# Dilated attention in a decoder trunk: both heads per query block, values stationary, output feature-major, one staging buffer

## The reference

```python
h = rmsnorm(x, g_mix)
qa, ka, va, qr, kr, vr, gr, ga, gb = split(h @ w_in)
# A: 3 groups x 8 heads of 64; windows (128,1), (512,4), (2048,16)
for each group: out_g, lse_g = dilated_group_attention(qa, ka, va)
y_A = (sum over groups of softmax(lse)_g * out_g) @ w_a
# B: retention, 4 heads, keys of 128, values of 256
y_B = (silu(gr) * groupnorm(retention(qr, kr, vr))) @ w_b
x = x + (sigmoid(ga) * y_A + sigmoid(gb) * y_B) @ w_o
x = x + square(relu(rmsnorm(x) @ w_up)) @ w_down
```

## Time and profile before

| what | value |
|---|---|
| median of 3 runs | 1989.29 us (1988.87 to 1989.97) |
| the profiled execution's own time | 1988.87 us |
| its span in the profile | 1987.1 us |
| PE busy | 1959.6 us, 99% of the span |
| mean granted clock of PE | 0.997 |
| DVE, ACT, POOL busy | 1106.3, 728.8, 90.7 us |
| DMA | 177.8 MB, 89 GB/s over the span |

### The profile page before, as it was taken

How to read it: one execution, slowest core, us unless ns; L and a number is a source line. 1 busy time by engine, 2 the same in 40 slices (tenths; PEclk the granted TensorE clock), 3 DMA queues, 4 the chain that set the end, 5 groups by cost and what they waited for, 6 DMA issues and landing times.

```text
span 1987.1 us, 26972 instructions
## 1 busy us (share of the span) xinstructions
PE 1959.6 (99%) x9580; PEld 1648.8 (83%) x9580; DVE 1106.3 (56%) x1716; ACT 728.8 (37%) x1146; POOL 90.7 (5%) x71
## 2 busy tenths in 40 slices
PE   7999999999999999999999999999999999999999
PEld 6988888887888888888889888888878888888887
DVE  5465664748446635354635474747564575445355
ACT  5144435355223413233422435344532233223233
POOL 0010110100000000000001110202000000000000
PEclk9999999999999999999999999999999999999999
DMA  5321222212333232322232222222122233232321
GB/s 173 111 91 44 89 69 84 84 51 76 100 101 106 86 106 87 103 98 92 98 117 91 81 74 63 90 63 90 35 95 95 95 106 106 85 106 84 106 85 64
DMA packets 203900, 177.80 MB, mean 89 GB/s; under 512 B 9776, under 2 KB 194224, under 8 KB 203568
## 3 DMA queue, kind: packets, MB, share of 16 engines
q1 hardware_dynamic: 203536, 176.52, 27.6%
q10 hardware_dynamic: 288, 0.28, 0.0%
HBM read 174.55 MB, written 2.23 MB: 89 GB/s over the span
## 4 chain that ended last, share of the span: by engine, by line
PE 81%; DVE 11%; issue 5%; ACT 2%; POOL 1%; DVEq 0%; DMA 0%; ACTq 0%; POOLq 0%; SPq 0%
PE pj L1155 21%; PE pj L1153 21%; PE pj L1154 21%; DVE w_lo L717 3%; DVE swp L809 2%; PE yo L1259 2%; PE rb L1286 2%; DVE swp L807 1%; DVE probT L878 1%; PE sc L1236 1%; PE pt L1246 1%; PE sc L1202 1%; PE sc L1204 1%; PE sc L1203 1%; PE rb L1272 1%
## 5 line engine op out<-in xcount | busy, mean ns | idle before, releaser
L1153 PE MATMUL pj<-h_hi,w_hi 128*128 128x512 f32 x1408 | 559.2, 397 | 0.0
L1155 PE MATMUL pj<-h_hi,w_lo 128*128 128x512 f32 x1408 | 548.6, 390 | 0.0
L1154 PE MATMUL pj<-h_lo,w_hi 128*128 128x512 f32 x1408 | 548.1, 389 | 0.0
L418 ACT CAST w_hi<-w_raw 128x1024 fp32r<-128x1024 f32 x330 | 329.9, 1049 | 371.0 <-PE pj L1155 277.6
L717 DVE TENSOR_TENSOR w_lo<-w_raw,w_hi 128x1024 fp32r<-128x1024 f32 x330 | 397.9, 1247 | 94.8 <-ACT w_hi L418 94.0
L1154 PEld LDWEIGHTS pj<-h_lo,w_hi 128*128 128x128 f32 x1408 | 264.5, 188 | 57.2 <-issue 2.4
L1153 PEld LDWEIGHTS pj<-h_hi,w_hi 128*128 128x128 f32 x1408 | 264.4, 188 | 56.6 <-issue 2.4
L1155 PEld LDWEIGHTS pj<-h_hi,w_lo 128*128 128x128 f32 x1408 | 264.2, 188 | 55.6
L1153 PE MATMUL pj<-z_hi,w_hi 128*128 128x512 f32 x640 | 249.6, 390 | 0.0
L1154 PE MATMUL pj<-z_lo,w_hi 128*128 128x512 f32 x640 | 249.2, 389 | 0.0
L1155 PE MATMUL pj<-z_hi,w_lo 128*128 128x512 f32 x640 | 249.2, 389 | 0.0
(11 more groups left out here) (185 smaller groups left out, 2348.4 us busy)
## 6 DMA issues: line engine op xcount, KB each, us to landing
w_raw<-in_w_in SPq DMA_DIRECT2D x152, 512.0 KB, 4.2
w_raw<-in_w_up SPq DMA_DIRECT2D x64, 512.0 KB, 4.1
w_raw<-in_w_down SPq DMA_DIRECT2D x64, 512.0 KB, 3.9
w_raw<-in_w_b SPq DMA_DIRECT2D x16, 512.0 KB, 3.8
w_raw<-in_w_o SPq DMA_DIRECT2D x16, 512.0 KB, 3.9
w_raw<-in_w_a SPq DMA_DIRECT2D x16, 256.0 KB, 3.0
x_nat<-in_x SPq DMA_DIRECT2D x2, 1024.0 KB, 6.4
tables<-in_tables SPq DMA_DIRECT2D x2, 1024.0 KB, 7.1
```

What stands on the lines that cost most here:

```text
L418: nc.scalar.copy(w_hi[s][:, c], raw[s][:, c]).then_inc(hi_done, 1)
L1153: nc.tensor.matmul(out, w_hi[s][:, wc], acts[0], start=first, stop=False)
L1154: nc.tensor.matmul(out, w_hi[s][:, wc], acts[1], start=False, stop=False)
L1155: return nc.tensor.matmul(out, w_lo[s][:, wc], acts[0], start=False, stop=last)
```

## The change

- **Both heads per query block.** A pass is now one query block with both heads: 4 passes j a pair. `prob`, `probT` and `pt` hold both heads. `masked`, `exp` work through 4 pieces each; `turn` makes 6 or 8 transposes; the passes are spread wider over the 12 steps (`turn(0)` now in step 5).
- **Values stationary.** `values` holds 64 columns of `vA` stationary and streams 128 columns of `probT`. Head 0 writes PSUM partitions 0 to 63, head 1 partitions 64 to 127, so the output is feature-major. The number of products is the same. `U` is feature-major and `u_copy` runs once for each block.
- **Statistics per pair.** After each pair SP exchanges that pair's residue statistics, DVE works out the shares (`shares`, `shares_end`, with an `Exp` on ACT, `share_power`, between), PE turns them to 4 rows with 4 small products (`share_rows`), ACT copies the rows (`rows_copy`), SP writes them to DRAM and reads them back broadcast over the partitions (`spread_rows`), and `y_sum` on DVE scales both sides of `U` and adds them.
- **Removed:** `factors`, `u_scale`, `y_turn`, `y_copy`, `y_add` at the gates.
- **One staging buffer.** `raw` is one buffer. A half of a unit is loaded once the same half of the unit before it has been split. In query/key units a half now holds one output tile, so that a tile needs its half alone.
- In PE's program the loop over the pairs is written out, which makes the column offsets of `vA` constants. The split of z, `ret_scale` and the gate copies are reordered at the gates. Retention's scratch moves from `prob` and `probT` to `scr`.

```diff
+            def load(n, halves, opens=None):
+
+                for i, (dst, src) in enumerate(halves):
+                    sp.wait_ge(lo_done, (n - 1) * 2 + i + 1 + UNIT_CREDIT)
+                    if opens and i == 0:
+                        sp.sem_inc(opens, 1)
+                    sp.dma_start(dst, src).then_inc(landed[i], 16)
...
+            def pair(v, *ts):
+
+                d = raw[:].rearrange("p (o k c) -> p o k c", o=2, c=P)
+                return [(d[:, o], v[:, :, t, :]) for o, t in enumerate(ts)]
...
+            def half_unit(n, v, t):
+
+                d = raw[:].rearrange("p (k c) -> p k c", k=KT)
+                sp.wait_ge(lo_done, (n - 1) * 2 + 1 + UNIT_CREDIT)
+                sp.dma_start(d[:, 0:KA, :], v[:, 0:KA, t, :]).then_inc(landed[0], 16)
+                sp.wait_ge(lo_done, (n - 1) * 2 + 2 + UNIT_CREDIT)
+                sp.sem_inc(landed[1], 16)
 
...
+                def exchange(J):
+
+                    sp.wait_ge(att_exp, J * 16 + 16)
+                    sp.dma_start(scratch.rearrange("(p r) c -> p r c", r=TB),
+                                 stats[:, TB:2 * TB].rearrange("p b w h -> p b (w h)")).then_inc(stats_sent, 16)
+                    sp.wait_ge(stats_sent, J * 16 + 16)
+                    sp.dma_start(other[:].rearrange("p b w h -> p b (w h)"),
+                                 scratch.rearrange("(b p) c -> p b c", p=P)).then_inc(other_in, 16)
+
+                def spread_rows(J):
+
+                    sp.wait_ge(rows_out, J + 1)
+                    sp.dma_start(row_scratch, rows).then_inc(rows_sent, 16)
+                    sp.wait_ge(rows_sent, J * 16 + 16)
+                    by_head = row_scratch.rearrange("(w h) s -> h w s", h=2)
+                    for hh in range(2):
+                        src = by_head[hh].unsqueeze(0).to_broadcast([DH, 2, S])
+                        sp.dma_start(spread_share[hh * DH:(hh + 1) * DH], src).then_inc(share_in, 16)
...
+                    last_two(i)
+                    after = first_four(l * LU + P0 + (i + 1) * P_U, w_in_next, i)
+                    load_pair(*after[0])
+                    load_pair(*after[1])
+                    exchange(J)
+                    load_pair(*after[2])
+                    load_pair(*after[3])
+                    spread_rows(J)
+                last_two(PAIRS - 1)
+
...
+                    load(n + 0, cols(w_in_u[l], COL_GA // 256 + p))
+                    load(n + 1, cols(w_in_u[l], COL_GB // 256 + p))
+                    if first:
+                        first()
+                    load(n + 2, cols(w_b_u[l], p))
+                    half_unit(n + 3, w_a_u[l], p)
+                    if last:
+                        last()
+
+                gates(0, lambda: exchange(l * PAIRS + PAIRS - 1), lambda: spread_rows(l * PAIRS + PAIRS - 1))
...
+                def share_power(J):
+                    act.wait_ge(share_diff, J * 3 + 3)
+                    nc.scalar.activation(share[:], share[:], ACT.Exp).then_inc(share_exp, 1)
+
+                def rows_copy(J):
+                    act.wait_ge(rows_turned, J + 1)
+                    nc.scalar.copy(rows, rb[0:4, :]).then_inc(rows_out, 1)
...
+                    ret_square(J, 0)
                     gate_sig(i, 1)
-                    act.wait_ge(att_pv, J * 8 + 8)
                     ret_square(J, 1)
+                    share_power(J)
                     rot_in(i + 1, 0, 0)
                     ret_root(J)
                     rot_in(i + 1, 0, 1)
-                    for u in range(1, GROUPS):
-                        ahead(l, P0, P_U, i + 1, u)
-                        rot_in(i + 1, u, 0)
-                        rot_in(i + 1, u, 1)
+                    ahead(l, P0, P_U, i + 1, 1)
+                    rot_in(i + 1, 1, 0)
+                    rows_copy(J)
+                    rot_in(i + 1, 1, 1)
+                    ahead(l, P0, P_U, i + 1, 2)
+                    rot_in(i + 1, 2, 0)
+                    rot_in(i + 1, 2, 1)
...
+                def u_copy(J, j):
+
+                    dve.wait_ge(att_pv, J * 4 + j + 1)
+                    if j == 0:
+                        dve.wait_ge(y_done, J + 1)
+                    c = slice(j * P, j * P + P)
+                    own, by_res = yo[:, 0:P], yo[:, P:2 * P]
+                    nc.vector.tensor_scalar(U[:, 0, c], own, 1.0, None, ALU.mult).then_inc(u_out, 1)
+                    nc.vector.tensor_scalar(by_residue(U[:, 1, :])[:, j], by_res, 1.0, None, ALU.mult).then_inc(u_out, 1)
...
+                def shares(J):
+
+                    own, res = stats[:, 0:TB], other[:]
+                    dve.wait_ge(other_in, J * 16 + 16)
+                    nc.vector.tensor_tensor(least[:], own[:, :, 0, :], res[:, :, 0, :], ALU.min).then_inc(share_diff, 1)
+                    dve.wait_ge(share_diff, J * 3 + 1)
+                    nc.vector.tensor_tensor(share[:, :, 0, :], least[:], own[:, :, 0, :], ALU.subtract).then_inc(share_diff, 1)
+                    nc.vector.tensor_tensor(share[:, :, 1, :], least[:], res[:, :, 0, :], ALU.subtract).then_inc(share_diff, 1)
+
+                def shares_end(J):
+
+                    own, res = stats[:, 0:TB], other[:]
+                    dve.wait_ge(share_exp, J + 1)
+                    nc.vector.tensor_tensor(own[:, :, 1, :], share[:, :, 0, :], own[:, :, 1, :], ALU.mult).then_inc(share_step, 1)
+                    nc.vector.tensor_tensor(res[:, :, 1, :], share[:, :, 1, :], res[:, :, 1, :], ALU.mult).then_inc(share_step, 1)
+                    dve.wait_ge(share_step, J * 4 + 2)
+                    nc.vector.tensor_tensor(least[:], own[:, :, 1, :], res[:, :, 1, :], ALU.add).then_inc(share_step, 1)
+                    dve.wait_ge(share_step, J * 4 + 3)
+                    nc.vector.reciprocal(least[:], least[:]).then_inc(share_step, 1)
+                    dve.wait_ge(share_step, J * 4 + 4)
+                    nc.vector.tensor_tensor(share[:], share[:], least[:].unsqueeze(2).to_broadcast([P, TB, 2, 2]),
+                                            ALU.mult).then_inc(share_done, 1)
+
...
+                def y_sum(i):
+
+                    J = l * PAIRS + i
+                    dve.wait_ge(u_out, J * 8 + 8 + 4)
+                    dve.wait_ge(share_in, J * 32 + 32)
                     for side in range(2):
...
+                        nc.vector.tensor_tensor(U[:, side, :], U[:, side, :], spread_share[:, side, :],
+                                                ALU.mult).then_inc(u_scaled, 1)
+                    dve.wait_ge(u_scaled, J * 2 + 2)
+                    nc.vector.tensor_tensor(y_of(i), U[:, 0, :], U[:, 1, :], ALU.add).then_inc(y_done, 1)
...
                     rotary(i, 3, 0)
                     masked(J, 0)
                     rotary(i, 3, 1)
+                    lo(n + 5, 1)
                     masked(J, 1)
-                    lo(n + 5, 1)
+                    st_decayed(J, 0)
                     masked(J, 2)
+                    st_decayed(J, 1)
+                    st_decayed(J, 3)
+                    u_copy(J, 0)
+                    lo(n + 6, 0)
                     masked(J, 3)
-                    st_decayed(J, 0)
-                    masked(J, 4)
-                    st_decayed(J, 1)
-                    masked(J, 5)
                     st_decayed(J, 2)
-                    lo(n + 6, 0)
-                    masked(J, 6)
-                    st_decayed(J, 3)
+                    u_copy(J, 1)
                     gate_scale(i, 0)
-                    masked(J, 7)
                     ret_copy(i, 0)
+                    u_copy(J, 2)
                     gate_scale(i, 1)
                     silu_gate(J, 0)
                     lo(n + 7, 1)
                     silu_gate(J, 1)
-                    u_copy(i)
+                    u_copy(J, 3)
                     ret_copy(i, 1)
                     ret_add(J)
+                    shares(J)
...
                     attend(i)
                     rotary(i + 1, 0, 0)
+                    shares_end(J)
                     rotary(i + 1, 0, 1)
                     ret_inverse(J)
                     lo(n + 8, 0)
                     ret_scale(i, 1)
                     rotary(i + 1, 1, 1)
                     lo(n + 9, 1)
+                    y_sum(i)
                     rotary(i + 1, 2, 0)
                     rotary(i + 1, 2, 1)
                 attend(PAIRS - 1)
...
                 g0 = l * LU + G0
+                last = l * PAIRS + PAIRS - 1
                 gate(0, 0, 0)
-                split_z(range(0, 4))
+                shares_end(last)
+                split_z(range(0, 6))
                 gate(0, 0, 1)
-                ret_inverse(l * PAIRS + PAIRS - 1)
+                ret_inverse(last)
+                lo(g0 + 2, 0)
+                gate(0, 1, 0)
                 ret_scale(PAIRS - 1, 0)
                 ret_scale(PAIRS - 1, 1)
-                split_z(range(4, 6))
-                lo(g0 + 2, 0)
-                gate(0, 1, 0)
-                factors()
```

(116 more changed lines are left out.)

384 lines of the change are left out of this document (142 added, 242 removed).

## The result

| | before | after |
|---|---|---|
| median | 1989.08 us (1988.37 to 1989.97, 4 runs) | 1976.19 us (1975.57 to 1976.80, 4 runs) |
| profiled execution | 1988.87 us, span 1987.1 | 1975.57 us, span 1973.8 |

The ratio is 0.9936, 95% interval 0.9924 to 0.9948: 12.9 us less, clear of the noise. The forecast was 1964 us with a range of 1955 to 1984. The time lies in the range, but half of the forecast gain of 25 us is missing.

A forecast was written before the change was run, and what follows sets the result against it. PE's own work plus a few waits bounds the kernel. Terms -24.0 + 12.8 + 7.0 - 7.0 - 11.9 - 1.9 = -25.0 from 1988.9 give 1963.9, forecast 1964 us, range 1955 to 1984.

The forecast's parts named there:

- A: Value products: two column halves run side by side, 30 slots of 0.11 us a pair for 60 records, 24.0 us saved.
- R1: Rival: the column halves do not run side by side, value products +2.4 instead of -24.0, 1990 us; chance 0.08.
- R2: Rival: stationary loads for half the columns stay in the open, value products 12.6 us a pair, 2038 us; chance 0.06.
- B: Changes of tile shape around `values` and `share_rows`: 8 a pair at 0.20 us each, 12.8 us added in all.
- C: `share_rows`: 4 float32 products, 8 records of 0.11 us, 0.9 us a pair, 7.0 us added in all.
- D: `y_turn` removed: 64 transposes of 0.11 us, 7.0 us saved.
- E: Start of the gates: PE's wait for `u_scale` and the clock's fall after it go, 11.9 us saved.
- three spares of about 1 us: At the gates: 0.8 us for `ret_root` before `share_rows`, 1.2 for the last z_lo tiles, 1.1 for y_lo.
- the 1 us that the prediction had named as a sign: No PE gap over 1 us between G0.1 and G0.3 at the gates, with the granted clock full there.
- R3: Rival: new waits at the gates, the clock falling again, and 0.5 us a pair for `exp` or the split, 1978 us; chance 0.17.
- F: `turn(0)` comes one step (2.9 us) later, so PE's 0.24 us wait for `exp` goes: 8 times, 1.9 us saved.
- At nothing: `y_sum`, shares, `share_power`, `exchange`, `spread_rows` and the single staging buffer cost PE nothing; 7.4 us remain for a 4.2 us load.

The follow-up runs named there:

- experiment 5: The kernel before with one staging buffer instead of two, loads waiting for both low halves of the unit before: 1989.40 us against 1989.44, ratio 1.0001.
- the first and the third version of experiment 1: The changed kernel with its padding mended (operands on multiples of 512 bytes), 1960.27 us; the changed kernel with z, m, y moved up 32 bytes, 1962.43 us.
- the two of experiment 4: Changed kernel with mended padding: three y splits moved ahead of the last y_sum, 1959.87 us; also the fourth unit's lo ahead and last split later, 1957.47 us.
- aligned kernel: The changed kernel with only its padding mended, so x, h, staging buffer, weights and tables start at multiples of 512 bytes like z, m, y: 1960.27 us.
- experiment 2: Changed kernel with mended padding: z, m, y moved up 64, 128, 256 bytes, 1968.48, 1977.75, 1960.23 us; or only w_lo and tables up 32 bytes, 2000.74 us.

## Why the prediction was right or wrong

What the forecast says for its own parts came out within 4 us; what it left out cost 16.6.

- **A, value products (-24.0): right.** In the changed kernel 16 records start in pairs 0.109 us apart, and a pass takes 1.02 us to the scores behind it, changes included:

```profile
329.70 0.60 PE L1313 MATMUL rb<-qkR 128*128 128x256 f32 x2
330.23 1.09 PE L1296 MATMUL yo<-probT,vA 128*64 128x128 f32 x16
331.25 1.15 PE L1270 MATMUL sc<-qk 64*128 64x256 f32 x12
```

  R1 is out, and so is R2. The rule that the prediction set against A (the Trainium skill, "TensorE: Matmul & The Clock Gate", The mechanism: stationary loads overlap products in flight only where the row group differs) does not hold here: both halves use all 128 rows, and two loads and two products fit in each 0.109 us. The Trainium skill's 2.38 for three column tiles on the same page (Measured speedup vs the span model) is 0.79 of full overlap; two halves here reach all of it, 60 records in 30 slots, a factor of 2.0.
- **B, changes of tile shape (+12.8): too dear by about 4.** Into the column halves costs 0.10 (329.70 plus two records of 0.21, to 330.23), not 0.20. From the halves to the scores it is 1.02 - 8 x 0.109 = 0.15, which stands in place of the 0.20 from full shape to scores that the kernel before paid. Back to full shape it is 0.26 (340.86 to 342.22 is 1.36, less 0.87 for the pass and 0.23 for a product). Two passes cost some 0.05 more than before, two 0.36, `share_rows` 0.30 (0.08 into it, 0.21 behind it): 1.1 a pair instead of 1.6. The measured pair agrees, 1.2 us less than before where 0.74 was forecast, 3.7 over 8 pairs.
- **C, share_rows (+7.0): right.** Its 8 records start 450.01 and the next product 450.98: 0.87 and the change.

```profile
449.70 0.39 PE L1182 MATMUL pj<-h_hi,w_lo 128*128 128x512 f32 x1
450.01 1.04 PE L1340 MATMUL rb<-ident,share 128*4 128x128 f32 x8
450.98 0.50 PE L1180 MATMUL pj<-h_hi,w_hi 128*128 128x512 f32 x1
```

- **D and E, y_turn and the wait (-18.9): right in the mechanism, 1.8 too good.** Neither the wait nor the clock's fall is left. Of the three spares of about 1 us that I had laid out, all held; the wait came at a fourth place that I had not laid out, the bank eviction behind the y splits, 0.71 us in the first layer and 1.06 in the second, there just over the 1 us that the prediction had named as a sign. That is R3's mechanism at a small part of its price, and the clock did not fall.
- **F (-1.9): right.** In the kernel before, `turn` waited for `exp` 8 times, 1.9 us in all; PE's waits in the changed kernel (below) have none for it.
- **At nothing.** The single buffer: right for PE where it stands alone (experiment 5). But the load is not covered as the prediction had it ("no wait of `w_hi` for a transfer"): in the changed kernel ACT stood idle for a transfer before a copy to `w_hi` 27 times, 57 us in all, where the kernel before has no such wait. None of PE's waits in its list for the changed kernel names a transfer but the first, for x. And the waits of PE at the first values of a layer fell from 4.8 + 1.8 + 0.5 us to 3.0 + 0.2, by 3.9, which was not forecast. That halves are now waited for one by one is a likely reason, but no run has it alone, and its size varies from trace to trace: the first and the third version of experiment 1 and the two of experiment 4 do not touch this place, and have 3.7, 4.8, 5.6 and 3.5 us there. Before, after, and ACT's largest sum of waits for a transfer:

```profile
PE sc L1202 <- DVE w_lo L717: 4.8, 2, 3.0
PE sc L1202 <- issue: 1.8, 1, 1.8
PE rb L1132 <- DVE h_lo L733: 0.5, 1, 0.5
```

```profile
PE sc L1150 <- DMA x_nat<-in_x: 6.8, 1, 6.8
PE sc L1230 <- DVE w_lo L748: 3.0, 2, 2.0
PE pj L1180 <- DVE sB L1038: 1.4, 2, 0.9
PE sc L1230 <- issue: 0.2, 1, 0.2
```

```profile
ACT w_hi L464 <- DMA w_raw<-in_w_in: 46.8, 23, 8.9
```

- **The step that failed** is the sum itself: it prices the edits and takes for granted that every product which the diff leaves alone keeps its duration. The changed small tensors at the front moved the weights 32 bytes against z, m and y: +16.6 us (2496 x 6.65 ns). The forecast would have needed the addresses of every operand of PE, before and after.

Put together for the aligned kernel: -25.0 - 3.7 (tile shapes) - 3.4 (starts of the layers, 7.1 to 3.7) + 2.5 (waits of 1.33 and 1.19) = -29.6, measured 1958.1 - 1987.1 = -29.0. With the offsets, for the changed kernel: -25.0 - 3.7 - 3.9 + 1.8 + 16.6 = -14.2, measured -13.3. So 0.6 and 0.9 us stay unexplained. That the changed kernel came near R3's 1978 us is luck: it did so for a reason that R3 does not name.

## What to carry to other kernels

After any edit that adds or drops a tensor, compare the mean duration of the products that were not edited, and the addresses of what PE reads: here a padding that a 32-byte rounding broke hid more than half of a real gain. Lay operands that PE reads together, both buffers of weights included, out on one offset modulo 256 bytes, and assert it in the code. A wait taken out of a tight order is worth only what the next one allows: the two reorderings had to be read one after the other from the trace.

## What the runs showed of the hardware

- A 128 x 512 product of float32r on z, m or y steps at 227 ns where moving and stationary operands stand at the same offset modulo 256 bytes (two runs shifted by 0 and 256, one with all 32 off), and at 229 to 234 ns at 32, 64, 96 and 128 bytes of difference; single lines go from 226 to 237 ns. Why is not shown. In the values' stage, where the stationary operand takes every fourth element of h, the step is 235.0 ns in the mean though the tensors stand at the same offset; for a stationary operand in one piece it is 227 to 228 ns there. Two weight buffers at different offsets slow down products that read none of the shifted bytes themselves, from 227 to 233 and 239 ns (experiment 2).
- Two column halves of the array, with all 128 rows in each, ran fully side by side, loads included: a pair of records each 0.109 us. With the heads one behind the other in the program, three records of the second still started before the last of the first.
- A change of tile shape is not symmetric: 0.10 us into the column halves, 0.26 back to the full array, 0.15 from the halves to the scores.
